# Block compression of a transformer layer in unsplit float32, in four column quarters of TensorE

## What is computed

```
def compress(t, j):                                  # j = 0: keys, 1: values
    blocks = t[:, blk_idx] + cmp_pos[j]              # 15 x 32 x 64
    hid = gelu(blocks.reshape(B, 15, 2048) @ phi_w1[j] + phi_b1[j])   # 2048 x 256
    return hid @ phi_w2[j]
kc, vc = compress(k_cmp, 0), compress(v_cmp, 1)
```

## Time and profile before

| | |
|---|---|
| median of 3 runs | 1299.21 us |
| profiled execution | 1297.27 us, its span 1295.4 us |
| TensorE matmuls busy | 1266.7 us, 98% of the span |
| TensorE weight loads busy | 1082.3 us, 84% |
| DVE / ACT / POOL busy | 840.3 / 683.7 / 236.7 us |
| granted TensorE clock | 1.00 throughout |
| chain that ended last | PE 87%, DVE 6%, issue 3%, ACT 2% |
| DMA | 222.65 MB, 172 GB/s on average |

### The profile page before, as it was taken

The page is one execution under the profiler, slowest core; times in us unless marked ns, Lnnn a source line. Parts: engine busy times, 40 slices in busy tenths (PEclk is TensorE's granted clock), DMA queues, the critical chain, the costliest instruction groups (busy, mean ns, idle before and its releaser), DMA issues.

```text
span 1295.4 us, 18623 instructions
## 1 busy us (share of the span) xinstructions
PE 1266.7 (98%) x6836; PEld 1082.3 (84%) x6836; DVE 840.3 (65%) x1175; ACT 683.7 (53%) x1111; POOL 236.7 (18%) x250
## 2 busy tenths in 40 slices
PE   7999999999999999999999999999999999999998
PEld 5888788799988878888878878888999898788886
DVE  5657957776657575555576588667866565655554
ACT  6455546565636554444464545564855455644442
POOL 1618911000002010000045297000000020100000
PEclk9999999999999999999999999999999999999999
DMA  9754554334524356555455555533254243655551
GB/s 337 262 190 153 186 191 147 146 115 163 171 91 179 130 197 221 178 188 194 162 182 192 194 181 180 186 146 141 92 195 164 98 159 130 233 185 182 177 189 65
DMA packets 32442, 222.65 MB, mean 172 GB/s; under 512 B 3584, under 2 KB 4096, under 8 KB 6784
## 3 DMA queue, kind: packets, MB, share of 16 engines
q1 hardware_dynamic: 30080, 209.28, 45.4%
q10 hardware_dynamic: 2304, 12.58, 2.5%
HBM read 219.75 MB, written 2.10 MB: 171 GB/s over the span
## 4 chain that ended last, share of the span: by engine, by line
PE 87%; DVE 6%; issue 3%; ACT 2%; DMA 1%; POOL 1%; SPq 0%; DVEq 0%; POOLq 0%; ACTq 0%
PE PS L1671 82%; DVE w_lo L1143 3%; PE PS L1786 1%; DMA raw<-in_weights 1%; PE PS L2000 1%; DVE x_lo L1146 1%; DVE work L1146 0%; ACT w_hi L666 0%; DVE PS L1143 0%; DVE rope_t L1314 0%; ACT x_hi L714 0%; DVE h L1146 0%; PE PS L1812 0%; PE PS L2050 0%; PE PS L2259 0%
## 5 line engine op out<-in xcount | busy, mean ns | idle before, releaser
L1143 DVE TENSOR_TENSOR w_lo<-raw,w_hi 128x1024 fp32r<-128x1024 f32 (+1 forms) x394 | 502.6, 1319 | 225.0 <-ACT w_hi L666 221.5
L666 ACT ACTIVATE w_hi<-raw 128x1024 fp32r<-128x1024 f32 x384 | 385.0, 1055 | 204.7 <-PE PS L1671 203.0
L1671 PE MATMUL PS<-w_hi,x_hi 128*128 128x512 f32 (+2 forms) x1104 | 425.3, 385 | 12.2 <-DVE x_lo L1146 6.2
L1671 PE MATMUL PS<-w_lo,x_hi 128*128 128x512 f32 (+2 forms) x1104 | 413.7, 375 | 0.0
L1671 PE MATMUL PS<-w_hi,x_lo 128*128 128x512 f32 (+2 forms) x1104 | 407.9, 375 | 0.0
L1671 PEld LDWEIGHTS PS<-w_hi,x_hi 128*128 128x128 f32 x1104 | 208.4, 189 | 53.9 <-issue 8.4
L1671 PEld LDWEIGHTS PS<-w_hi,x_lo 128*128 128x128 f32 x1104 | 208.3, 189 | 38.4
L1671 PEld LDWEIGHTS PS<-w_lo,x_hi 128*128 128x128 f32 x1104 | 208.7, 189 | 34.8 <-issue 0.5
L1671 PE MATMUL PS<-w_hi,hid_hi 128*128 128x512 f32 (+1 forms) x368 | 139.2, 381 | 0.0
L1671 PE MATMUL PS<-w_lo,hid_hi 128*128 128x512 f32 (+1 forms) x368 | 138.2, 380 | 0.0
L516 POOL TENSOR_SCALAR st<-st 128x1 f32<-128x1 f32 x32 | 20.8, 651 | 619.4 <-ACT proj L689 550.8
(11 more groups left out here) (277 smaller groups left out, 1335.9 us busy)
## 6 DMA issues: line engine op xcount, KB each, us to landing
raw<-in_weights SPq DMA_DIRECT2D x194, 1024.0 KB, 4.7
pmat<-in_mats ACTq DMA_DIRECT2D x3, 1664.0 KB, 8.1
gain<-in_post ACTq DMA_DIRECT2D x8, 512.0 KB, 3.6
zone<-mem_scratch ACTq DMA_DIRECT2D x2, 1024.0 KB, 6.5
raw<-in_weights SPq DMA_DIRECT2D x3, 512.0 KB, 7.4
h<-in_x SPq DMA_DIRECT2D x2, 512.0 KB, 6.1
zone<-in_mem SPq DMA_DIRECT2D x1, 1024.0 KB, 10.5
mem_scratch<-zone ACTq DMA_DIRECT2D x1, 1024.0 KB, 8.9
```

The costliest lines, as they stand in the source:

```text
L666: a.activation(w_hi[s][:, c_], raw[s][:, c_], ACT.Copy).then_inc(sem[hi_done[s]], 1)
L1143: return v.tensor_tensor(o, x_, y_, op)
L1671: return t_.matmul(o, a_, b_, start=first, stop=last)
```

## The change

Block units are no longer split. The blocks stay in float32 in `zone`, and TensorE reads the float32 weights straight from `raw`. Each of the 8 row tiles of a unit is one float32 matmul with 256 moving columns. It takes 32 stationary columns from `zone`: the 15 of its block tile and 17 that belong to the following ones. Row tile k writes the 32 partitions from 32 (k mod 4) on of bank 0, so four row tiles in a row go to four quarters of the bank, and the four partial sums are added in the fold, which now contracts over 128 partitions with four identities of 15 in 32 rows.

With that go, per layer: four ACT splits and four DVE splits, the two ACT copies and two DVE subtractions that split the blocks, and ACT's wait for `phi_h`. DVE's copy of the sums has 128 partitions, not 30. The slot of a block unit is free for the next load when TensorE is done with it (`unit_done`), not after a split, and TensorE waits for the landing (`raw_in`). `bl` moves 32 columns down, and POOL clears the last 48 columns of `zone` once at the start, since the last tiles' 32 columns reach into them. The rest is counting: semaphores of splits count only split units.

```diff
 def slot_of(u, l):
-    return (u + l * N_UNITS) % SLOTS, u // SLOTS
+    return (u + l * N_UNITS) % SLOTS, u // SLOTS, sum(v - 3 * FU not in PHI_UNITS for v in range(u % SLOTS, u, SLOTS))
...
-    k[:2 * NC_CMP, K_FOLD:K_FOLD + NC_CMP] = np.tile(np.eye(NC_CMP), (2, 1))
+    k[:, K_FOLD:K_FOLD + NC_CMP] = np.tile(np.eye(32, NC_CMP), (4, 1))
...
-        bl = v3(zone[:, 7696:8176], "p (j k n) -> p j k n", j=2, k=CMP_KT)
+        bl = v3(zone[:, 7664:8144], "p (j k n) -> p j k n", j=2, k=CMP_KT)
...
                 for m in range(N_MID):
                     s, n, ns = mid(l, m)
-                    sp.wait_ge(*E.at(split_done[s], ns))
+                    if m - SLOTS in PHI_UNITS:
+                        sp.wait_ge(*E.at(unit_done[s], n))
+                    else:
+                        sp.wait_ge(*E.at(split_done[s], ns))
                     load(s, 3 * FU + m)
...
+            pool.memset(zone[:, 8144:8192], 0.0)
...
-                act.wait_ge(*E.at("blocks_done", 1))
-                for j in range(2):
-                    i = a.activation(blocks[j][:, :, 0:NC_CMP], bl[:, j], ACT.Copy)
-                i.then_inc(sem["blocks_hi"], 1)
-                split_mid(11)
...
-                split_mid(13)
                 split_mid(14)
...
-                split_mid(16)
...
-                split_mid(18)
...
-                act.wait_ge(*E.at("phi_h", 1))
...
-                dve.wait_ge(*E.at("blocks_hi", 1))
-                for j in range(2):
-                    i = tt(blocks[j][:, :, NC_CMP:2 * NC_CMP], bl[:, j], blocks[j][:, :, 0:NC_CMP].bitcast(F32), ALU.subtract)
-                i.then_inc(sem["blocks_done"], 1)
...
-                v.tensor_copy(phi_rows[0:2 * NC_CMP], bank(0)[0:2 * NC_CMP]).then_inc(sem["phi_h"], 1)
+                v.tensor_copy(phi_rows, bank(0)).then_inc(sem["phi_h"], 1)
...
                 def phi_unit(q):
-                    s, _, ns = mid(l, PHI_UNITS[q])
+                    s, n, _ = mid(l, PHI_UNITS[q])
                     j, half = q // 2, q % 2
-                    pe.wait_ge(*E.at(split_done[s], ns + 1))
-                    o = bank(0)[:, j * UC:(j + 1) * UC]
+                    pe.wait_ge(*E.at(raw_in[s], 16 * (n + 1)))
                     for k in range(KT):
-                        b_ = blocks[j][:, half * KT + k]
-                        wh, wl = (w[s][:, k * UC:(k + 1) * UC] for w in (w_hi, w_lo))
-                        first, last = half == 0 and k == 0, half == 1 and k == KT - 1
-                        if first:
-                            mm(o[0:2 * NC_CMP], b_, wh, True, False)
-                        mm(o[0:NC_CMP], b_[:, 0:NC_CMP], wl, False, False)
-                        if not first:
-                            i = mm(o[0:2 * NC_CMP], b_, wh, False, last)
+                        at = 7664 + (j * CMP_KT + half * KT + k) * NC_CMP
+                        i = mm(bank(0)[32 * (k % 4):32 * (k % 4) + 32, j * UC:(j + 1) * UC], zone[:, at:at + 32],
+                               raw[s][:, k * UC:(k + 1) * UC], half == 0 and k < 4, half == 1 and k >= 4)
                     i.then_inc(sem[unit_done[s]], 1)
...
-                    i = mm(bank(0)[:, q * 16:q * 16 + NC_CMP], phi_rows[0:2 * NC_CMP, q * P:(q + 1) * P],
-                           con[0:2 * NC_CMP, K_FOLD:K_FOLD + NC_CMP], True, True)
+                    i = mm(bank(0)[:, q * 16:q * 16 + NC_CMP], phi_rows[:, q * P:(q + 1) * P],
+                           con[:, K_FOLD:K_FOLD + NC_CMP], True, True)
```

More of the change, by code:

```diff
@@ L58, in slot_of @@
 def slot_of(u, l):
-    return (u + l * N_UNITS) % SLOTS, u // SLOTS
+    return (u + l * N_UNITS) % SLOTS, u // SLOTS, sum(v - 3 * FU not in PHI_UNITS for v in range(u % SLOTS, u, SLOTS))
 SLOT_USES = [len(range(s, N_UNITS, SLOTS)) for s in range(SLOTS)]
+SPLITS = [sum(v - 3 * FU not in PHI_UNITS for v in range(s, N_UNITS, SLOTS)) for s in range(SLOTS)]
 _at = 0
@@ L267, in program @@
         phi_rows = rope_t[:, 256:768]
-        blocks = [v3(x_[:, 0:2 * NC_CMP * CMP_KT], "p (k n) -> p k n", k=CMP_KT) for x_ in (hid_hi, hid_lo)]
         s5_tiles = [v3(x_[:, :], "p (i s) -> p i s", i=2) for x_ in (hid_hi, hid_lo)]
@@ L285, in program @@
         raw_in = [signal(f"raw_in{s}", 16 * SLOT_USES[s]) for s in range(SLOTS)]
-        hi_done = [signal(f"hi_done{s}", 2 * SLOT_USES[s]) for s in range(SLOTS)]
-        split_done = [signal(f"split_done{s}", SLOT_USES[s]) for s in range(SLOTS)]
+        hi_done = [signal(f"hi_done{s}", 2 * SPLITS[s]) for s in range(SLOTS)]
+        split_done = [signal(f"split_done{s}", SPLITS[s]) for s in range(SLOTS)]
         unit_done = [signal(f"unit_done{s}", SLOT_USES[s]) for s in range(SLOTS)]
@@ L298, in program @@
                 mla_xn=1, mla_t1=1, mla_t1c=1, mla_qkv=1, mla_nope=1, mla_tok=1, mla_t2=1, mla_qt=1, mla_kt=1,
-                nsa_rope=2, nsa_v=1, nsa_t=2, nsa_tc_act=1, nsa_tc_dve=1, blocks_done=2, blocks_hi=1,
+                nsa_rope=2, nsa_v=1, nsa_t=2, nsa_tc_act=1, nsa_tc_dve=1, blocks_done=1,
                 phi_h=1, phi_t=1, phi_x=1, phi_th=1, phi_hid=1, phi_out=1, phi_c=1,
@@ L352, in mid @@
         def mid(l, m):
-            return *slot_of(3 * FU + m, l), slot_of(3 * FU + m, l)[1]
+            return slot_of(3 * FU + m, l)
         def ffn_unit(l, f, role, i=0):
             du, i0 = dict(first=(0, 0), second=(1, 0), a=(2, 1), b=(3, 1), down=(4, 0), last=(3 * FU - 1, 0))[role]
-            s, n = slot_of(FFN_AT[f] + du, l)
-            return s, i + (n - i0), i + (n - i0)
+            s, n, ns = slot_of(FFN_AT[f] + du, l)
+            return s, i + (n - i0), i + (ns - i0)
         FILL = [0, 16, 32, 40, 48, 56, 60]
@@ L2129, in _ @@
                 kv_half(2, 0)
-                pe.wait_ge(*E.at("blocks_done", 2))
+                pe.wait_ge(*E.at("blocks_done", 1))
                 pe.wait_ge(*E.at("xkv_done", 1))
```

## The result

The changed kernel takes 1290.97 us (median of five runs, 1290.7 to 1294.61), the kernel before, measured beside it, 1299.21 (1296.78 to 1302.17). My forecast of 1300.1 was wrong, and its rival (a), four at once, is what happened. A second measurement, further down, gives 1294.21 and a ratio of 0.9962 (0.9949 to 0.9974).

The account below looks back on a forecast made before the run. TensorE's order of work was taken as the bound. Terms 64t - 14.9 + 3.1 - 0.6 - 2.6 + 0.4, with 64t = 15.5, gave +0.9 on 1297.27, plus 1.94 for the median: 1300.1 us, range 1292.5 to 1303.5.

Parts of the forecast that it names:

- rival (a): Block units on TensorE: all four quarters stream at once, 0.86 us a unit; sum -5.6, so 1293.6 us; chance 0.28.
- What bounds the kernel: TensorE, busy 1266.7 of 1295.4 us: its order of work is the time, with one exponentials wait per layer between block units.
- Part 1: Block-unit matmuls on TensorE: 14.9 us removed, 64 float32 matmuls added; program order gives nine instruction times, 1.94 us a unit.
- 64t: Total of the 64 added float32 matmuls, t being one matmul's time in a unit: 15.5 us forecast.
- Part 2: Mode changes around TensorE's block units: 0.39 us a visit, eight visits, 3.1 in all (lower bound 1.6); fold saves 0.6.
- Part 3: Splits dropped from ACT and DVE: third attention group's exponentials come 1.33 us earlier, -1.3 a layer, -2.6 in all.
- the likely case: Block units in program order with pairs overlapping: 1297.5 to 1303 us, chance 0.48; nothing left of the wait for the exponentials.
- Part 4: Loads wait for TensorE to finish block units: unit 19 just hidden, unit 21 late by 0.2 us a layer, +0.4.
- Unit 21's 0.4: Scores of the last group wait for unit 21's later load and split: +0.2 us a layer, +0.4 in all.
- (b): Block units on TensorE: quarters run one after another, t stays 0.431; sum +12.6, so 1311.8 us; chance 0.16.
- rival (c): Loads of units 19 and 21 land in 5.5 us, not 4.7: +3.2, so 1303.3 us; late loads or another wait 0.08.
- The sum: All terms for the whole kernel: 64t - 14.6, giving +0.9 us on the profiled execution and a forecast median of 1300.1 us.

Follow-up runs that it names:

- second measurement: The changed kernel, unaltered, run again beside eleven runs of the kernel before (1297.8): 1294.21 us, ratio 0.9962 (0.9949 to 0.9974).
- the eight widths: Changed kernel with a unit's eight matmuls given 256 down to 200 moving columns, results not the block's; only unit times read, no total given.
- the run with the moves: Changed kernel plus ACT's table load early, squares and unit 19's split before ACT's copy, first block unit beside the transposes: 1290.5 us, ratio 0.9937.

## Why the prediction was wrong

**What bounds the kernel: right.** TensorE is busy for 98% of the span, and every part of the gain is either a shorter stretch of it or one of its waits.

**Part 1, the time of one matmul: the step that failed.** I wrote that matmuls start in program order in every row, "so only the second instruction of one matmul and the first of the next can stream together", and took t = 0.242, 64t = 15.5. The four batches of 0.216, and 0.024 more for the first, make 0.89 a unit and 64t = 7.1. The rows I had were all of matmuls that used all columns, or the same ones; an order seen there says nothing about quarters. The instruction time of 0.215 itself was right, and with it both bounds: from the first to the last start of a unit one quarter takes 3.26 us, fifteen steps of 0.216 and 0.02, and four take 0.69, three such steps and 0.04. The rule of the Trainium skill that I leaned on, "TensorE: Matmul & The Clock Gate", Part 3, that matmuls on different tiles start and end strictly in program order, doesn't hold for the starts of this case's column tiles: the eight widths show a start ahead of three earlier matmuls. Of the ends no run here tells. What the Trainium skill says in "TensorEngine Tiling (Array Packing)", Key Properties, that tiles work independently, is what the runs show.

**Part 2, the visits: right in kind, too large.** 0.28 each, 2.3 in all, for 0.39 and 3.1; my lower bound was 0.2. The steps of 0.09 at the first start and 0.10 behind were there. Of the 0.20 inside, half was not: the scores of the earlier trace rows, with 64 rows of contraction, have 0.32 from their first start to their second where 0.216 is the step, and a block unit, with 128 rows and 32 columns, has 0.240. The nearest neighbours were not the same kind of visit. The fold: 0.5 for 0.6.

**Part 3, the wait for the exponentials: right.** 0.6 to 0.7 should stay in case (a), 0.62 did. With the splits kept it is 1.95, which gives the 1.33. In the likely case nothing should stay, and with two quarters nothing did.

**Part 4, the loads: one right, one missed without a price.** In case (a) TensorE was to reach unit 19 0.5 before DVE had it: it is 0.68, with the loss in (a) put at 1.1 and measured at 1.36. Unit 21's 0.4 was not there, as (a) has it. It was there with two quarters, 0.48 in both layers, and with one, 0.44, where (b) took it off: there (b) is wrong by that much. But of two loads that now start 0.4 apart the second takes up to 8.17 us (unit 20: 338.88 to 347.06), where the longest before took 5.5; my rival (c) was too mild. It cost nothing only because those units had the time. In the run with the moves the first load of such a pair took 5.52 and did decide.

**The sum.** Rival (a) said -5.6 against the profiled execution; it was -6.3. Its terms with measured numbers: 7.1 - 14.9 + 2.3 - 0.5 - 2.6 + 1.2 + 1.4 = -6.0, and 0.35 from a wait in layer 0 that I had not counted. The rest of the distance between its 1293.6 and the measured 1290.97 is the 1.94 that I put on top, for the median of three runs of the kernel before; the changed kernel's profiled execution was its median. In the second measurement the changed kernel took 1294.21, which lies in my range and 0.6 from (a)'s number. To be right by that would have been luck, since the rule of order behind the range's middle was wrong all the same. The chance of 0.28 for (a) was too low: one rule for it and one against, with no row of this trace on either side, called for nearly even chances and a range down to about 1290.

## What to carry to other kernels

Float32 matmuls that need at most 32 stationary columns can run four at a time when their outputs go to the four 32-partition quarters of a bank. With 256 moving columns each then costs a quarter of its full-width time, and a group of them a fixed 0.28 us for the way into the mode and out of it: here it beat a three-product float32r form of 16 matmuls, and took its splits off two engines as well. Whether float32r gains in quarters was not tried. Order seen between full-width instructions is no evidence for instructions that use separate parts of an engine; where a rule has no row behind it, give both outcomes their price and nearly the same chance. When TensorE gets shorter, ask at each wait what the waited-for engine itself follows. What follows TensorE's work behind the shorter piece moves along with it, as the maxima behind unit 11 do. A chain that begins ahead of the shorter piece keeps its length and turns into the next stall, as the copy, the split and the subtraction of unit 19 behind the transposes do; a load or another engine's order can hold it up further. Idle time ahead of a load is where work with nothing to wait for belongs.

## What the runs showed of the hardware that I had not expected

- Column quarters behave as if each had a queue of its own, for float32: matmul 7 of a unit started before 4, 5 and 6, and four instructions deep nothing in one quarter held up another.
- It follows that a signal on the last matmul of such a group need not be the last to finish; with equal widths the last four start 6 to 8 ns apart. The trace models the ends, so no run here shows an early signal; that is argued, not shown. With equal widths the records of a batch can't be told apart, so that the last of the program is then the last to finish isn't shown either.
- One, two and four quarters: 3.57, 1.85 and 1.00 us for the same sixteen instructions of 256 columns, the way out included. There is no loss from sharing the moving side.
- Between float32 and float32r at full width there is no cost at either end, and none for float32r with 30 columns; float32 with 32 columns costs 0.28 us a visit.
- Of two loads of 1 MB that start 0.4 us apart the first took 4.6 to 4.8 us in layer 0 of the changed kernel, about as long as one alone, and the second 6.7 to 8.2.
- TensorE's granted clock fell to 1.2 GHz for a few us in some executions and not in others of the same kernel at the same place. A stretch of 6.8 us cost some 3 us, half of this change, and one of 3.4 us some 1.6. Time and mean clock of the runs go together: six runs of the changed kernel go from 1291.72 at 0.998 to 1297.46 at 0.994, so this is most of their scatter.
